# Two seven-product pairs instead of one in the last three feed-forward stages, with the token sums moved from GpSimd to VectorE

## The reference, cut to what matters

```
def swiglu(x, w_in, w_out):
    gate, up = jnp.split(x @ w_in, 2, axis=-1)
    return (jax.nn.silu(gate) * up) @ w_out
...
x = x + 0.5 * swiglu(rms_norm(x, ffn1_norm_g[i]), ffn1_w_in[i], ffn1_w_out[i])
...
def swiglu_2(h, w_gate, w_up, w_down):
    return (jax.nn.silu(h @ w_gate) * (h @ w_up)) @ w_down
```

## Time and profile before

| | us |
|---|---|
| median of 3 runs | 1532.05 (1531.9 to 1535.41) |
| the profiled execution's own time | 1531.57 |
| its span in the trace | 1529.8 |
| granted TensorE clock, mean | 0.999 |
| stages 0 to 4, from the start of D 0 to that of D 9 | 56 to 201, 372 to 519, 554 to 699, 840 to 984, 1367 to 1511 |

### The profile page before, as it was taken

How to read it: one execution, slowest core, us unless ns; L and a number is a source line. 1 busy time by engine, 2 the same in 40 slices (tenths; PEclk the granted TensorE clock), 3 DMA queues, 4 the chain that set the end, 5 groups by cost and what they waited for, 6 DMA issues and landing times.

```text
span 1529.8 us, 19935 instructions
## 1 busy us (share of the span) xinstructions
PE 1517.7 (99%) x7906; PEld 1292.2 (84%) x7906; DVE 1094.3 (72%) x1174; ACT 858.6 (56%) x1075; POOL 358.5 (23%) x256
## 2 busy tenths in 40 slices
PE   9999999999999999999999999999999999999998
PEld 7888888888778888888888888899988899888886
DVE  6677766557778567776776678599998566666875
ACT  7545554645365454556776456476887343464554
POOL 0352200001732135320001631100571000017320
PEclk9999999999999999999999999999999999999999
DMA  7977665457776688765416986766554665578763
GB/s 253 314 243 233 188 182 188 138 170 211 239 246 192 193 275 251 228 195 173 158 56 206 285 230 203 209 191 204 181 181 147 212 192 187 173 223 273 226 194 102
DMA packets 274309, 311.43 MB, mean 204 GB/s; under 512 B 64272, under 2 KB 233512, under 8 KB 274216
## 3 DMA queue, kind: packets, MB, share of 16 engines
q1 hardware_dynamic: 273112, 308.84, 64.4%
q10 hardware_dynamic: 1104, 1.31, 0.3%
HBM read 295.92 MB, written 1.09 MB: 194 GB/s over the span
## 4 chain that ended last, share of the span: by engine, by line
PE 90%; POOL 3%; DVE 2%; issue 2%; DMA 2%; ACT 2%; ACTq 0%; DVEq 0%; POOLq 0%
PE ps L2344 22%; PE ps L2348 22%; PE ps L2345 22%; PE ps L2334 3%; PE ps L2336 3%; PE ps L2335 3%; PE ps L2546 2%; PE ps L2545 2%; PE ps L2544 2%; DMA scr<-scr 1%; PE ps L2387 1%; PE ps L2500 1%; POOL scr L750 1%; DVE w_lo L1412 1%; POOL scr L760 0%
## 5 line engine op out<-in xcount | busy, mean ns | idle before, releaser
L1412 DVE TENSOR_TENSOR w_lo<-w_raw,w_hi 128x2048 fp32r<-128x2048 f32 x250 | 598.5, 2400 | 185.1 <-ACT w_hi L803 184.7
L803 ACT ACTIVATE w_hi<-w_raw 128x2048 fp32r<-128x2048 f32 x250 | 477.0, 1912 | 250.8 <-PE ps L2348 200.5
L2344 PE MATMUL ps<-w_hi,xg_hi 128*128 128x512 f32 (+1 forms) x960 | 375.2, 391 | 1.2 <-DVE scr L1527 1.2
L2348 PE MATMUL ps<-w_hi,xg_lo 128*128 128x512 f32 (+1 forms) x960 | 372.1, 388 | 0.0
L2345 PE MATMUL ps<-w_lo,xg_hi 128*128 128x512 f32 (+1 forms) x960 | 372.0, 387 | 0.0
L750 POOL COPY scr<-scr 128x512 uint16<-128x512 uint16 x100 | 121.1, 1231 | 697.8 <-DVE scr L1527 697.7
L2344 PE MATMUL ps<-w_hi,y_hi 128*128 128x512 f32 x666 | 261.9, 393 | 1.3 <-DVE y_lo L1532 0.7
L2348 PE MATMUL ps<-w_hi,y_lo 128*128 128x512 f32 x666 | 259.1, 389 | 0.0
L2345 PE MATMUL ps<-w_lo,y_hi 128*128 128x512 f32 x666 | 258.9, 389 | 0.0
L2344 PEld LDWEIGHTS ps<-w_hi,xg_hi 128*128 128x128 f32 x960 | 180.3, 188 | 39.1 <-DVE w_lo L1412 1.6
L2348 PEld LDWEIGHTS ps<-w_hi,xg_lo 128*128 128x128 f32 x960 | 180.3, 188 | 36.8
(11 more groups left out here) (403 smaller groups left out, 1710.8 us busy)
## 6 DMA issues: line engine op xcount, KB each, us to landing
w_raw<-in_ffn_w_in_dram SPq DMA_DIRECT2D x168, 512.0 KB, 5.0
w_raw<-in_ffn_w_out_dram SPq DMA_DIRECT2D x88, 512.0 KB, 5.5
w_raw<-in_w_in_dram SPq DMA_DIRECT2D x82, 512.0 KB, 4.6
w_raw<-in_a_w_in_dram SPq DMA_DIRECT2D x28, 512.0 KB, 4.5
w_raw<-in_w_down_dram SPq DMA_DIRECT2D x22, 512.0 KB, 5.1
w_raw<-in_w_gate_dram SPq DMA_DIRECT2D x21, 512.0 KB, 4.1
w_raw<-in_w_up_dram SPq DMA_DIRECT2D x21, 512.0 KB, 5.2
y_raw<-in_ffn_w_in_dram SPq DMA_DIRECT2D x16, 512.0 KB, 5.4
```

The costliest lines, as they stand in the source:

```text
L803: act.activation(w_hi[:, u % RING, :], w_raw[:, u % RING, :], ACT.Copy).then_inc(w_rounded, 1)
L1412: dve.tensor_tensor(w_lo[:, s, :], w_raw[:, s, :], w_hi[:, s, :].bitcast(F32), ALU.subtract).then_inc(w_split, 1)
L2344: pe.matmul(dst, xh, hi, start=start, stop=False, skip_group_check=True)
L2348: return pe.matmul(dst, xl, hi, start=False, stop=stop, skip_group_check=True)
```

## The change

A table gives the pairs of each stage: at step 8 in stages 0 and 1, at steps 4 and 8 in stages 2, 3 and 4. The places of the units in the order follow from it. The x and S sums are made on VectorE, in the step three ahead of the first pair. T1, T3 and T2 of a pair are made in a row: behind the products two steps ahead of the first pair, and for a pair at step 8 that follows one at step 4, near the end of the first pair. T4 is made one step ahead, the low part of T2 at the start of the pair. The extra transfers move accordingly. The pieces of the diff are, in this order: the table and the order of the units, a step in SyncE's queue, GpSimd, a step on VectorE, the x sum there, and a pair on VectorE.

```
+PAIRS_OF = ((8,), (8,), (4, 8), (4, 8), (4, 8))
...
         if i in pairs:
+            order += [("G", i, 0), ("G", i, 1), ("G", i + 1, 1), ("D", i - 1), ("G", i + 2, 0), ("G", i + 2, 1), ("D", i), ("D", i + 1)]
...
                 def step(i):
+                    p = pairs[0]
+                    gate_up(1, i)
+                    if i == p - 2:
+                        block(p, 1, 1)
+                    down(i - 1)
+                    if i == p - 3:
+                        block(p, 0, 0)
...
+                    if i < NI - 1:
+                        gate_up(0, i + 1)
+                    turn_back(i - 1)
+                    if i == p - 3:
+                        block(p, 0, 1)
+                        block(p, 1, 0)
+                    if i == p - 2:
+                        block(p, 2, 0)
+                        block(p, 2, 1)
...
-                    if i == 1:
-                        x_sums()
-                    if i == 2:
-                        s_sums()
...
                     split(v + 2)
+                    hidden_low(i - 1, (i - 1) % 2)
-                    if i == 3:
-                        t_sum(T1, T3, T1, "T1")
-                    if i == 4:
-                        t_sum(T3, T2, T3, "T3")
-                    if i == 5:
-                        t_sum(T4, T4, T2, "T4")
-                    if i == 6:
-                        t_low(T2)
+                    if i == pairs[0] - 3:
+                        x_sums()
+                    if i + 1 in pairs:
+                        t_sum(i + 1, T4, T4, T2, "T4", "T2")
                     split(v + 3)
                     for tt in range(2):
                         product(i, tt)
...
+                    if i == pairs[0] - 3:
+                        s_sums()
+                    if i + 2 in pairs:
+                        t_sums(i + 2)
+                    if i + 1 in pairs:
+                        t_low(i + 1, T1)
+                    if i + 1 == pairs[0]:
+                        s_lows((0, 1))
                     split(v + 4)
...
+                def x_sums():
+
+                    dve.tensor_tensor(x_sum, xg_hi[:, :, :].bitcast(F32), xg_lo[:, :, :].bitcast(F32), ALU.add).then_inc(vec_done, vec(f"X {f}"))
...
                     n = u + at["G", p, 0]
+                    t_low(p, T2)
                     split(n + 2)
+                    if p == pairs[0]:
+                        s_lows((2, 3))
...
                     split(n + 8)
+                    if p + 4 in pairs:
+                        t_sums(p + 4)
...
                     split(n + 9)
```

More of the change, by code:

```diff
@@ L346, in build, with alone_until, alone @@
         T1, T3, T2, T4 = range(4)
+        def alone_until(f, i):
+            def alone(f, j):
+                return j not in PAIRS_OF[f] and j - 1 not in PAIRS_OF[f]
+            return sum(alone(g, j) for g in range(f) for j in range(NI)) + sum(alone(f, j) for j in range(i + 1))
         x_sum = tiles(KB(40, 8))
@@ L1636, in ffn @@
                     pass
[L1637 to L1641 removed]
+                i = 3
+                while i < NI:
+                    if i in pairs:
+                        pair(i)
+                        i += 3
+                    else:
+                        step(i)
+                        i += 1
             def mem(n, gain, factor):
```

399 lines of the change are left out of this document (206 added, 193 removed).

## The result

| | before | after |
|---|---|---|
| median of 4 runs each, side by side, us | 1533.29 (1531.90 to 1535.41) | 1546.88 (1546.86 to 1547.99) |
| ratio to before, 95% interval | | 1.0089 (1.0072 to 1.0107) |
| the profiled execution's own time, its span | 1531.57, 1529.8 | 1547.99, 1546.1 |
| granted TensorE clock, mean | 0.999 | 0.996 |

I had forecast 1532.2 us, 1524 to 1539, no change. The median went up by 13.6 us, 0.9%, and the interval of the ratio lies wholly above 1; the two profiled spans differ by 16.3 us.

A forecast was written before the change was run, and what follows sets the result against it. The kernel was taken to be bound by TensorE's stream of matmuls. 1531.57 - 8.2 (three blocks) - 2.3 (stage 1's waits) + 10.6 (new waits for VectorE) = 1531.7, with 0.5 for the median 1532.2 us; range 1524 to 1539.

The forecast's parts named there:

- The gains: On TensorE: three blocks of matmuls removed, 8.2 us, and two waits of stage 1 freed, 2.3 us; together 10.5 us.
- No wait at D 1: TensorE waiting for hidden values at D 1 was named as a sign that the forecast was wrong; no size given.
- The work of VectorE's row alone: VectorE's instructions from step p-2's products to T2's low part (p: first pair), without GpSimd's contention: 25.1 us.
- The end of the products: Step p-2's products, counted from X, D p-3's start: X + 1.2 in stages 0, 1; X + 2.9 in 2, 3; X + 1.9 in 4.
- the size of the stretch, 27.3 us: VectorE from step p-2's products to M6 at first pairs: 25.1 row, 1.2 cuts, 1.0 joins, against TensorE's 27.2 us.
- The joins: Two GpSimd joins in VectorE's crowded stretch, taken to cost VectorE 0.5 us each.
- VectorE without idle time in this row: Sign of being right: VectorE never idle from step p-2's products to T2's low part, 26.5 to 28 us.
- my own formula: M6 at first pairs waits by (end of step p-2's products - X) + 27.3 - 27.2; sum 10.6 us.
- the second pair at 0: At the pair of step 8 in stages 2 to 4: no wait, cost 0, bound 0.6 us in each stage.
- every new wait of TensorE adds to the time in full: TensorE's matmul stream being the bound, each new wait was to add its length; no clock loss was counted.
- Rival 3: Slower, by port turns: each GpSimd copy holds unpaused VectorE for its whole length, 2.9 us more per stage, 1546.6 us; chance 0.09.
- Rival 4: Slower, by queue: full 1.8 us on stages 2 to 4's transpose, x and S sums' 1 us passed on; 1537.9 us; chance 0.11.

The follow-up runs named there:

- e7_short_copies: Changed kernel with GpSimd's copies in steps 1 to 9 cut down, a cut to a quarter and a join to an eighth of its words; 1532.9 us.
- e13_short_copies_s_high: Changed kernel with GpSimd's cuts at a quarter and joins at an eighth of their words, and ScalarE's S highs a step earlier; 1528.8 us.
- e6_early_transfers: Changed kernel with the transfers of the second pair's T blocks 0 to 2 issued inside the first pair; 1555.6 us.
- e10_t1_early: Changed kernel with T1's sum, high and low part taken out of VectorE's crowded row and the S highs early on ScalarE; 1526.8 us.
- e5_s_high_early: Changed kernel with ScalarE making the four S highs a step earlier, behind the silus of step p-2 (p: first pair); 1541.0 us.
- e3_sums_behind_split: Changed kernel with the three T sums ahead of a first pair placed behind the split of G p-1,1 (p: first pair); 1551.3 us.
- e2_first_pair_only: Changed kernel with only the pair at step 4 kept in stages 2 to 4, the one at step 8 removed; 1550.7 us.

## Why the prediction was wrong

**Right.** The gains: 36 matmuls fewer, and stage 1's two waits gone. Where the new waits stand, and on which instructions. No wait at D 1. The work of VectorE's row alone: 25.1 us, which e7_short_copies measured as 25.1 in stages 0 and 1, and e13_short_copies_s_high in stages 0 to 2. The end of the products in stages 0 and 1 (X + 1.19), and nearly that in stages 2 and 3 (X + 3.45 and 2.70 for 2.9); stage 4 came to X + 2.71 instead of 1.9.

**Wrong, first: the size of the stretch, 27.3 us.** It was 27.0, 28.1, 28.3, 29.9 and 29.9. Two terms failed. The joins were set at 0.5 us each, from a row in which VectorE had been waiting when the join began; in an unbroken row a join costs 1.1. The Trainium skill's rule that I had weighed and put at 0.09 ("SBUF — State Buffer", section "Who interferes with whom") came nearer for the joins, and its 30.2 us for the stretch is near the 29.9, though not for its reason: the copies together cost 1.9 us in stage 0, 3.0 in stage 1 and 3.2 in stages 2 to 4, where whole turns would be 5.1. The rest, 1.5 us in stages 3 and 4, is VectorE's wait for ScalarE, which my sum did not have at all. I had followed VectorE's row and asked who comes in its way, and never asked whether what it waits for, rounding by rounding, was there in time. Nor had I followed the transpose of step p-2's values, whose data GpSimd waits for 1.5 to 1.8 us longer in stages 3 and 4 than in stage 0. One of my own signs of being right, VectorE without idle time in this row, failed in these two stages.

With the measured numbers in my own formula (products' end + stretch - 27.2) the waits are 1.0, 2.1, 4.5, 5.4 and 5.4, in sum 18.4, and 18.1 were measured, for 10.6 forecast. Of what is over, the stretch makes 6.7 us and the later end of the products 1.1. The formula held, its inputs didn't.

**Wrong, second: the second pair at 0.** It cost 2.8 us in waits at M6. The step that failed is "T4 and the low parts of this pair have two steps with nothing else in them; they cost nothing". I had looked at the split behind the sums, which came in time, and not at the transpose of step 6, which stands in the queue behind four T transfers. e6_early_transfers shows it: with them elsewhere the transpose is issued in 1.2 to 2.0 us and VectorE's row to M6 is 0.9 to 2.3 us shorter. It takes both, the late transpose and the work behind it: in e10_t1_early the transpose is still late, but T1's low part stands ahead of the wait, and M6 is in time. How much of the 2.8 us is the queue's is not exact, since e5_s_high_early, with the same queue, has 1.8.

**Wrong, third: the clock, which the prediction puts at nothing.** The step was "every new wait of TensorE adds to the time in full": two of the waits brought the half clock with them and added more than their length. It cost 4.6 us by the starts behind M6 (5.1 us in my expectations, which took the whole length of both half-clock stretches and so counted part of the wait itself).

**The balance.** 1529.8 - 8.2 - 2.3 + 18.1 + 2.8 + 4.6 = 1544.8 us, and the span was 1546.1. Of the missing 1.3 us about half is the 0.1 to 0.2 us that TensorE is late behind each wait at the full clock too, as in the second start at 871.94, 0.34 us behind the first; the rest I did not trace.

**My rivals.** Rival 3 gave the best time (1546.6), and that is luck: it had 14.4 us more by whole turns on the port, and the copies cost only some 3.5 us more than my sum had, in five stages together; what made up the time, ScalarE, the second pairs and the clock, it did not have. Rival 4, the queue, was real, but at the transposes of step p-2 and of step 6, and not, or little, where I put it. Together they had a chance of 0.2, and both stood on one side of a sum that had no slack left, 27.3 us of work for 27.2.

**Still open.** Whether TensorE's clock falls is not decided by the length of one wait: it fell after 2.13 us at M6 (stage 0 of e3_sums_behind_split) and after 2.27 (stage 3 of e5_s_high_early), and not after 2.26 (stage 4 there), nor after 3.32 at M6 (stage 4 of e3_sums_behind_split), nor after 3.37 at G 3,1 (stage 2 of the changed kernel), while it did after 3.25 in the same place in e2_first_pair_only. Also open is why the transpose of step p-2 is back later in stages 3 and 4: no run moved only what is in flight beside it.

## What to carry to other kernels

Work moved onto an engine that is 72% busy on average must be fitted into the stretch between two deadlines, with every copy beside it at its full price, and the other engines' queues must be walked through the same stretch: a row that is full on paper waits on whoever feeds it. Take work out to where the engine waits anyway: the same change costs 13.6 us with T1 and the S highs in the row, and the kernel is 7.3 us faster than before with them ahead of it. Test the better order without the new work too: of these 7.3 us the three extra pairs bring only 2.3. Where one queue carries loads and transposes, the place of each transfer decides, and a move that frees one transpose can hold up another.
